# Mixer weights are split into high and low parts once and kept in DRAM, in a kernel for a hybrid decoder block

## What is computed

```python
xn = rmsnorm(h, norm1_g[l])
proj = jnp.einsum('bsd,de->bse', xn, w_in[l])
# columns of proj: q, k (256 each), v, g (512 each), z (16), c_in, c_gate (512 each)
o_gla = gla_chunked(q, k, v, log_a)                 # recurrence over chunks of tokens
o_gla = rmsnorm(o_gla, gla_norm_g[l]).reshape(B, S, GLA_VAL) * jax.nn.silu(g)
u = c_in * jax.nn.sigmoid(c_gate)
u = causal_depthwise_conv(u, conv_w[l], conv_b[l])  # 31 taps along the tokens
o_conv = jax.nn.silu(channel_group_norm(u, conv_norm_g[l], conv_norm_b[l]))
mixed = jnp.concatenate([o_gla, o_conv], axis=-1)
h = h + jnp.einsum('bse,ed->bsd', mixed, w_out[l])
```

## Time and profile before

| | before |
|---|---|
| median of 3 runs | 2590.87 us (2590.35 to 2591.17) |
| span of the profiled execution | 2587.6 us |
| mixer, from the span's start | 0 to 1124 us |
| MLP | 1124 to 2587.6 us |
| PE busy, share of the span | 89% |
| DVE, ACT, POOL busy | 52%, 31%, 40% |

### The profile page before, as it was taken

How to read it: one execution, slowest core, us unless ns; L and a number is a source line. 1 busy time by engine, 2 the same in 40 slices (tenths; PEclk the granted TensorE clock), 3 DMA queues, 4 the chain that set the end, 5 groups by cost and what they waited for, 6 DMA issues and landing times.

```text
span 2587.6 us, 29357 instructions
## 1 busy us (share of the span) xinstructions
PE 2302.8 (89%) x10192; PEld 1864.8 (72%) x10192; DVE 1350.7 (52%) x2373; ACT 790.2 (31%) x1166; POOL 1040.2 (40%) x878
## 2 busy tenths in 40 slices
PE   7768867896799768869999999999999999999998
PEld 6546656664576557548888888888778888888887
DVE  4956677749593958533434343434643333333335
ACT  3335534352436333531121212121422221212122
POOL 5575576656764686432222222222432222222222
PEclk9988978997899889879999999999999999999999
DMA  4212212322232212362111111112151111111111
GB/s 126 64 49 58 74 39 73 123 53 62 78 102 70 57 53 86 107 230 62 49 49 49 49 49 49 49 49 81 50 195 49 49 49 49 48 49 43 54 32 65
DMA packets 177335, 179.00 MB, mean 69 GB/s; under 512 B 8896, under 2 KB 140000, under 8 KB 177248
## 3 DMA queue, kind: packets, MB, share of 16 engines
q1 hardware_dynamic: 177248, 177.93, 22.3%
HBM read 161.13 MB, written 16.78 MB: 69 GB/s over the span
## 4 chain that ended last, share of the span: by engine, by line
PE 53%; DVE 2%; ACT 1%; DMA 1%; POOL 0%; SPq 0%; issue 0%; POOLq 0%; ACTq 0%
PE ps L67 9%; PE ps L69 9%; PE ps L68 9%; PE ps L1661 9%; PE ps L1663 9%; PE ps L1662 9%; DVE hn L1561 1%; DVE h_sb L1598 0%; DVE hT_lo L1570 0%; POOL m_rstd L1454 0%; ACT m_junk L1505 0%; DMA hn<-h_dram 0%; SPq L1404 0%; DVE h_sb L1576 0%; DMA h_sb<-h_dram 0%
## 5 line engine op out<-in xcount | busy, mean ns | idle before, releaser
L1458 POOL TENSOR_TENSOR m_lo<-raw,m_hi 128x1024 fp32r<-128x1024 f32 x128 | 305.9, 2409 | 1029.2 <-ACT m_hi L1514 1029.0
L595 POOL TENSOR_TENSOR w_lo<-w_raw,w_hi 128x512 fp32r<-128x512 f32 x224 | 399.6, 1795 | 345.4 <-ACT w_hi L694 345.2
L1598 DVE TENSOR_TENSOR h_sb<-ps,h_sb 128x512 f32<-128x512 f32 x512 | 350.1, 690 | 273.3 <-PE ps L1663 269.8
L891 DVE SCALAR_TENSOR_TENSOR y_sb<-u_sb,cw_col,y_sb 128x512 f32<-128x512 f32 x480 | 406.6, 914 | 3.5 <-issue 3.3
L67 PE MATMUL ps<-hT_hi,m_hi 128*128 128x512 f32 x1024 | 399.9, 391 | 7.3 <-POOL m_lo L1458 4.2
L1661 PE MATMUL ps<-m_hi,ff_hi 128*128 128x512 f32 x1024 | 400.3, 391 | 6.1 <-DVE h_sb L1598 5.4
L1663 PE MATMUL ps<-m_hi,ff_lo 128*128 128x512 f32 x1024 | 399.5, 390 | 0.0
L1662 PE MATMUL ps<-m_lo,ff_hi 128*128 128x512 f32 x1024 | 399.4, 390 | 0.0
L68 PE MATMUL ps<-hT_lo,m_hi 128*128 128x512 f32 x1024 | 399.3, 390 | 0.0
L69 PE MATMUL ps<-hT_hi,m_lo 128*128 128x512 f32 x1024 | 399.3, 390 | 0.0
L1585 DVE TENSOR_TENSOR relu<-relu 128x512 f32<-128x512 f32 x128 | 88.6, 692 | 484.1 <-ACT relu L1521 484.1
(11 more groups left out here) (167 smaller groups left out, 3097.0 us busy)
## 6 DMA issues: line engine op xcount, KB each, us to landing
w_raw<-in_w_in SPq DMA_DIRECT2D x160, 256.0 KB, 2.8
raw<-in_w_mlp_in SPq DMA_DIRECT2D x64, 512.0 KB, 4.2
raw<-in_w_mlp_out SPq DMA_DIRECT2D x64, 512.0 KB, 3.3
w_raw<-in_w_out SPq DMA_DIRECT2D x64, 256.0 KB, 2.8
hn<-h_dram SPq DMA_DIRECT2D x16, 512.0 KB, 5.9
h_sb<-h_dram SPq DMA_DIRECT2D x16, 512.0 KB, 7.3
out_h<-h_sb SPq DMA_DIRECT2D x16, 512.0 KB, 2.6
x_nat<-in_x SPq DMA_DIRECT2D x14, 512.0 KB, 5.0
```

Source lines behind the costliest of these rows:

```text
L595: nc.gpsimd.tensor_tensor(w_lo[:, slot, :], w_raw[:, stage, :], w_hi[:, slot, :].bitcast(F32), ALU.subtract).then_inc(w_lo_ok, 1)
L891: nc.vector.scalar_tensor_tensor(out=y_sb[:, j, :], in0=u_sb[:, j, k:k + BLK], scalar=cw_col[:, j, k:k + 1], in1=y_sb[:, j, :], op0=ALU.mu ...
L1458: nc.gpsimd.tensor_tensor(m_lo[:, i, :], raw[:, i, :], m_hi[:, i, :].bitcast(F32), ALU.subtract).then_inc(m_lo_ok, 1)
L1598: nc.vector.tensor_tensor(h_sb[:, t, c], ps[:, 4 + n % 4, :], h_sb[:, t, c], ALU.add).then_inc(add_ok, 1)
```

## The change

A unit's two parts are made once, at its first use. The two parts now lie beside each other in one tile `wt`, and when the split is done SP stores both (512 KB) into a DRAM tensor `w_kept`. When the same weights come up again for a later token block, SP loads both parts from `w_kept` straight into the slot, and neither ACT nor POOL touches them. 56 units are new, 168 are loaded again. New units are the first 40 (block -1 and block 0 up to `g`) and the 16 `out` units of block 1. PE waits for the split on a new unit and for the load's own semaphore `w_again` on a kept one. The load of a kept unit is issued when its slot is free, four units ahead of its use; the raw load of a new one is still issued eight ahead. ACT's copy into a slot also waits until the store out of that slot has landed.

Since different blocks now have different work, the loop over blocks 1 and 2 is written out, and all counts are constants. DVE's small copies into `pace` (line 877, one ahead of each predicated copy in `gla_select`, 256 in all) are taken out.

```diff
+FIRST_UNITS = FRONT_UNITS + OUT_UNITS
...
-        pace = sb("pace", [P, 1])
...
-        w_hi = sb("w_hi", [P, SLOTS, UNIT], F32R)
-        w_lo = sb("w_lo", [P, SLOTS, UNIT], F32R)
+        wt = sb("wt", [P, SLOTS, 2, UNIT], F32R)
+        w_hi, w_lo = wt[:, :, 0, :], wt[:, :, 1, :]
+        w_kept = nc.dram_tensor("w_kept", [FIRST_UNITS, P, 2, UNIT], F32).ap()
...
+        w_st = [sem(f"w_st{i}") for i in range(SLOTS)]
+        w_again = [sem(f"w_again{i}") for i in range(SLOTS)]
...
-            with eng.Fori(1, NB - 1) as b:
+            for b in MIDDLE:
...
+        def is_new(n):
+
+            return n < LAST_UNIT and KEPT_AT[UNITS[n][0]] == n
+
+        def is_kept(n):
+            return n < LAST_UNIT and not is_new(n)
...
+            def store_new(n):
+                i = nth_new(n)
+                sp.wait_ge(w_lo_ok, i + 1)
+                sp.dma_start(w_kept[i], wt[:, n % SLOTS, :, :].bitcast(F32)).then_inc(w_st[n % SLOTS], 16)
+
+            def load_kept(n):
+
+                first_n = KEPT_AT[UNITS[n][0]]
+                sp.wait_ge(w_st[first_n % SLOTS], stores_in_slot(first_n) * 16)
+                sp.wait_ge(w_used, n - SLOTS + 1)
+                if is_new(n - SLOTS):
+                    sp.wait_ge(w_st[n % SLOTS], stores_in_slot(n - SLOTS) * 16)
+                sp.dma_start(wt[:, n % SLOTS, :, :].bitcast(F32), w_kept[nth_new(first_n)]).then_inc(w_again[n % SLOTS], 16)
 
             def load_ahead(b, i):
 
...
+                n = base(b) + i
+                if is_new(n + SLOTS + STAGES):
+                    load_new(n + SLOTS + STAGES)
+                if is_new(n + SLOTS):
+                    store_new(n + SLOTS)
+                elif is_kept(n + SLOTS):
+                    load_kept(n + SLOTS)
...
             def split_next(b, i):
 
-                n = i + SLOTS
-                if isinstance(b, int) and base(b) + n >= LAST_UNIT:
-                    return
-                split_lo(base(b) + n, n % SLOTS, n % STAGES)
+                if is_new(base(b) + i + SLOTS):
+                    split_lo(base(b) + i + SLOTS)
...
-            def carry_wait():
-
-                nc.vector.tensor_copy(pace[:, :], one_col[:, :])
...
             def weights(b, i):
-                pe.wait_ge(w_lo_ok, base(b) + i + 1)
+                n = base(b) + i
+                if is_new(n):
+                    pe.wait_ge(w_lo_ok, nth_new(n) + 1)
+                else:
+                    pe.wait_ge(w_again[n % SLOTS], loads_in_slot(n) * 16)
```

More of the change, by code:

```diff
@@ L375, in mixer_block, with run @@
         BODY = block_steps(True, True)
+        MIDDLE = range(1, NB - 1)
         END, LAST = last_steps(block_steps(True, False))
         def base(b):
-            if isinstance(b, int) and b <= 0:
+            if b <= 0:
                 return 0 if b < 0 else CONV_UNITS
-            return b * BLOCK_UNITS if not (isinstance(b, int) and b == NB) else NB * BLOCK_UNITS - OUT_UNITS
-        def run(eng, do):
+            return b * BLOCK_UNITS if b < NB else NB * BLOCK_UNITS - OUT_UNITS
+        def run(do):
             for s in FIRST:
@@ L402, in first @@
         def first(b):
[L403 removed]
+            return b <= 0
         def out_bank(b, half, t):
@@ L444, in sources @@
                 elif name == "out":
                     half, k = step[1]
-                    out += [w_out_t[:, k, half * 512:half * 512 + 512]]
+                    out += [((name, half, k), w_out_t[:, k, half * 512:half * 512 + 512])]
             return out
-        STREAMS = [sources(steps) for steps in (FIRST, START, BODY, END, [s for s, _ in LAST])]
-        assert [len(u) for u in STREAMS] == [CONV_UNITS, FRONT_UNITS, BLOCK_UNITS, OUT_END, OUT_UNITS]
+        STREAMS = [sources(steps) for steps in (FIRST, START, *([BODY] * len(MIDDLE)), END, [s for s, _ in LAST])]
@@ L452, in _, with nth_new, stores_in_slot, loads_in_slot @@
+        def nth_new(n):
+            return FIRSTS.index(n)
+        def stores_in_slot(n):
+            return sum(1 for m in FIRSTS if m <= n and m % SLOTS == n % SLOTS)
+        def loads_in_slot(n):
+            return sum(1 for m in range(n % SLOTS, n + 1, SLOTS) if is_kept(m))
         @block.sync
         def _(sp):
[L454 to L458, removed]
+            def load_new(n):
+                i = nth_new(n)
+                if i >= STAGES:
+                    sp.wait_ge(w_lo_ok, i - STAGES + 1)
+                src = UNITS[n][1]
+                dst = w_raw[:, i % STAGES, :]
@@ L533, in _ @@
             sp.dma_start(cw_col[:, :, :], conv_w).then_inc(consts_ld, 16)
-            for n in range(STAGES, STAGES + SLOTS):
-                load(n, STREAMS[0][n], n - STAGES + 1)
-            run(sp, do)
+            for n in range(SLOTS):
+                load_new(STAGES + n)
+                store_new(n)
+            run(do)
         @block.gpsimd
@@ L680, in _ @@
                     make_plain()
-            for g in range(SLOTS):
-                split_lo(g, g, g)
+            for n in range(SLOTS):
+                split_lo(n)
             make_zero_parts()
@@ L712, in x_sq @@
                     act.wait_ge(x_norm, (b - 1) * TT + t + 1)
-                    if not (isinstance(b, int) and b == 1):
+                    if b > 1:
                         act.wait_ge(cn_f, (b - 1) * CT)
@@ L1050, in _ @@
             dve.wait_ge(made, MADE)
-            run(dve, do)
+            run(do)
         @block.tensor
@@ L1276, in _ @@
                 x_tr(0, t)
-            run(pe, do)
+            run(do)
 CONSTS = 16 * (1 + 2 + 4 + 1)
```

101 lines of the change are left out of this document (45 added, 56 removed).

## The result

The changed kernel takes 2458.55 us (median of 4 runs, 2455.05 to 2464.16) against 2590.61 us (2581.24 to 2591.17) for the kernel before: ratio 0.9503, 95% interval 0.948 to 0.9527. That is 132 us less. The prediction was 2517 us with a range of 2490 to 2562, so the sign was right and the gain nearly twice as large as foreseen. The profiled execution took 2464.16 us with a span of 2462.4 us.

A forecast was written before the change was run, and what follows sets the result against it. The prediction saw the mixer bound by PE's idle 242 us, with waits for POOL's splits held behind DVE taps, and the lower clock. Terms 27 + 12 + 15 + 14 + 6 + 0 = 74 us gave 2517 us, range 2490 to 2562.

The forecast's parts named there:

- item 4: Starts of blocks 1 to 3: PE's waits for `cum` shrink as taps no longer share with splits; 14 us gained.
- item 2: POOL's chunk ahead of the transposes, blocks 1 to 3: splits and ACT copies leave `silu_g`'s chain; 12 us gained.
- item 1: `v` units of blocks 1 to 3: PE's stall for the held split shrinks, first scores come sooner; 27 us gained.
- item 3: Behind `out`: PE's waits for late splits go, with their restarts; 15 us gained, bounds 8 to 18.
- item 6: `LAST`: the 4.24 us stand goes, but the ninth unit's load follows the residual load; 0 us, bounds -4 and +7.
- Item 7: What is added, kept loads, stores and the loop written out: cost 0, up to 5 us lost from the loop.
- Item 5: The 256 DVE copies into `pace` taken out: 6 us gained, bounds 0 and 39.
- A: The forecast, chance 0.58: the stall shrinks by what POOL's chunk gets faster and the tied waits go; 2517 us.
- C: Rival, chance 0.10: `k_end` is not held but alternates with taps, and PE stands at the second scores; 2505 us.
- B: Rival, chance 0.20: longer runs of taps hold other POOL work, such as `mix_lo`, `rstd` or `qe`; 2553 us.
- D: Slower rival, chance 0.06: kept loads land late, above 7.8 us, and PE waits on each unit; 2769 us at 9.3.
- E: Rival, chance 0.03: the chunk chain, DVE and the transposes take the saving back; time stays within 0.2%.

The follow-up runs named there:

- a_both: The changed kernel with POOL's subtraction and ACT's copy of the old splits done again for 128 kept units, results unused and nobody waiting: 2549.44 us.
- a_gap: The changed kernel with one DVE fill of 128 x 1 behind every fourth tap: 2457.14 us.
- u_gap: The program that splits every unit (loop written out, no `pace`, 2582.32 us) with one DVE fill of 128 x 1 behind every fourth tap: 2579.64 us.
- a_twice: The changed kernel with each of 128 kept units loaded a second time, into a spare buffer PE does not wait for: 2462.66 us.
- a_last: The changed kernel with the second half's residual load in `LAST` issued behind the first half's last `out` units: 2453.52 us (ratio 0.9488).
- the five with stand-ins: The changed kernel with unused POOL and/or ACT instructions put back at places of kept units' old splits: 2532.39, 2472.84, 2549.44, 2474.13 and 2491.35 us.

## Why the prediction missed

**The step that failed is the price of the splits for which PE did not wait: item 4 above all, then item 2.** The sum was 74 us and the mixer became 124.6 us shorter. Of the 50.6 us between them 20.2 are item 4's and 15.5 item 2's; 6.4 are item 1's, 4.2 item 3's, 5.0 `LAST`'s and 5.2 those of blocks -1 and 0, less some 6 for `pace`, which gave almost nothing. The method behind it went from wait to wait: each item was a wait that a split ended, priced along the one chain that led to it. a_both shows what that leaves out. With PE free of all splits, the work that they took from POOL, DVE and ACT costs 72.4 us between `z` and the end of `out`, where 72.1 had been gained.

**Item 4** (14 forecast, 34.2 measured) counted some 16 splits and 0.85 us on each tap that they meet. There are 11 splits in block 2's stretch alone and 32 in the three blocks. They also slowed what else DVE read from SBUF with two operands (`fac`: 944 ns against 283), left DVE with four taps of the time before, and each stand had a low-clock stretch behind it, which only items 1, 3 and 6 had priced. 32 times the same 0.85 would have been 27. Block 2's 14.6 us hold some 2.7 of the loop.

**Item 1** (27, 33.4; its better bound was 35) came out near its number, and its signs are all in the trace: `k_end` is held in the split's place, PE stands 11.4 to 12.7 us at the first scores and nowhere in `v`. The first scores came 13.1 to 14.2 us sooner, somewhat more than the 8 to 12 that the forecast allowed itself, and PE's restart behind them took 2.2 to 2.8 us of that back, where 2.7 was forecast. But the chain that it follows, held instruction, POOL's chunk, first scores, is not what sets the length. In a_gap POOL's chunk of block 2 is through 13 us earlier (19.4 us behind the start of `v` and not 32.7) and the stretch up to the transposes is the same to 0.5 us; in u_gap the held split itself is let in, and the stretch is 0.7 to 2.2 us longer. So the number was near partly by luck: what DVE and POOL do together up to the second scores was about as long as the chain, and was relieved by the same splits.

**Item 2** (12, 27.5): it counted two splits and four copies on one chain, 4.8 us a block. In blocks 2 and 3 a_both gives back 12.3 and 10.3 us of the 12.7 and 11.3 there, and block 3, in which I counted half, gained as much as block 2. **Item 3** (15, 19.2) is the one place where a wait was a price: a_both gives back nothing of block 2's 9.4. It was too low since block 1 gained as much as block 2; the unit that was late is the second convolution unit of the next block, which is kept in block 1 too. **Item 6**: the ninth unit came 2.8 us late as forecast (2 to 6), but the place was 5.0 us shorter all the same: PE's wait at the channel norm ahead of it fell from 7.79 to 5.57 us, and the unit had waited 4.24 before. **Item 7**: no cost, as said; the loop gave 5 us. **Item 5**: about 1 and not 6.

**The rivals.** A's signs appeared but for one: `k_end` held for 18.31 and 19.54 us, 11.4 to 12.7 us at the first scores, `silu_g` at 9.2 and 5.8 (7 forecast), `cum` below 3, one late kept unit, the MLP as before. The taps did not come near 0.7 us: 369.6 us for 480 are 0.77 each. The right picture with a wrong account of the time. C did not occur, and where it was forced (a_gap) the stretch up to the transposes changed by 0.5 us at most and not by 4 a block. Of B's holds there is one, an `o_sb` of 7.03 us at 304.07 in block 1. PE did not wait for it: that stretch from `z` to `v` took 28.87 us with it and, in a_gap, without it. The `mix_lo` took 2.8 us at most. D is out by a factor of two in traffic (a_twice). E fell.

**What stays open.** Block 1's 32.9 us had no stand-ins; that they have the same cause rests on the table under u_gap, not on a run of its own. Neither had the 5.2 us of blocks -1 and 0. Why ACT's copies cost 4.1 us already in block 2 was not taken apart; they are between `z` and `v` (2.9) and behind the second scores (2.7), less 1.4 in `v`.

## What to carry to other kernels

Where two engines share access and both feed the one that waits, do not sum the waits: lay the stretch between two fixed points side by side with the work of both engines in it, and price a removed instruction by what it took from both (here 0.56 us per subtraction, 0.7 with ACT's copy, over 128 places, though most of them had no wait behind them). A wait is a price by itself only where nothing else would be late, as behind `out`, where PE is busy for 60.30 of 60.30 us once it is gone. Before a stall is priced, ask what would be late if it were gone; a run that frees the waiting instruction without removing it (a tiny instruction in the long run of the other engine) answers that. Count every instruction in a window of the trace, not along one chain.

## What the runs showed of the hardware

**A hold lasts for the whole run, and a 0.06 us instruction ends it.** In the changed kernel block 0's split (25.59 us) and the three `k_end` (18.31, 19.54 and 19.54) came into a run of two-input DVE taps and ended 0.6 to 1.1 us behind its last tap. How far into the run they came does not explain it: block 0's came 2.1 us in, and before the change a split that came 12.6 us into block 3's run of 14 taps took 1.84:

```profile
865.82 1.84 POOL L595 TENSOR_TENSOR w_lo<-w_raw,w_hi 128x512 fp32r<-128x512 f32 x1 [1.85 <-ACT w_hi L694]
```

In the traces of the kernel before, the changed kernel and a_last, what differs is how long POOL had stood before. With 3 us or more of a run of taps left, every instruction that was held had 4.85 us or more of standing ahead of it, and every one that came 3 us or more into the run and was let in had 3.2 us or less. That is an observation; no run varied it by itself. With a DVE fill of 128 x 1 behind every fourth tap (59 ns each) no POOL instruction of the mixer took more than 2.3 us in a_gap, and none more than 4.24 in u_gap. The Trainium skill (SBUF — State Buffer, SBUF: two separate sides) gives the shared pair for one whole instruction; by that rule `k_end` should have waited for one tap of 0.665 us. The trace does not agree for these back-to-back taps, and does where a fill stands between them.

**Who is let in can hang on some microseconds, and block 0 then has two lengths.** In a_last's profiled execution a split of block 0 came at 116.05 and took 1.42 us:

```profile
116.05 1.42 POOL L634 TENSOR_TENSOR wt<-w_raw,wt 128x512 fp32r<-128x512 f32 x1 [1.80 <-ACT wt L734]
```

In the changed kernel's, with the same program up to there:

```profile
117.24 25.59 POOL L634 TENSOR_TENSOR wt<-w_raw,wt 128x512 fp32r<-128x512 f32 x1 [5.25 <-ACT wt L734]
```

Block 1 begins at 288.7 us in the one and at 297.14 in the other, a difference about as wide as the spread of the changed kernel (2455.05 to 2464.16). Nine of the profiled programs have the same block 0 (changed kernel twice, a_last, a_twice and the five with stand-ins): eight were held for 25.59 us and begin block 1 between 294.3 and 297.2 us, and only a_last was let in. That this is what makes the changed kernel's spread was not shown, since one execution of each was profiled.
